# The weight rings start at the activations' offset within 512 bytes: 288 unused bytes ahead of them

## What is computed

```python
for l in range(DEPTH):                        # DEPTH = 2
    h = rms_norm(x, norm_mix[l])
    proj = h @ w_in[l]                        # 1024 x 5120
    ...
    x = x + mixed @ w_out[l]
    h = rms_norm(x, norm_ffn[l])
    x = x + conv_ffn(h, w_up[l], conv_w[l], conv_b[l], w_down[l])
x = rms_norm(x, norm_final)
proj = rmsnorm(x, norm_mix_w_2) @ w_in_2
...
x = x + mix @ w_out_2
u = relu(rmsnorm(x, norm_mlp_w_2) @ w_ff1_2)
x = x + (u * u) @ w_ff2_2
return rmsnorm(x, final_norm_w_2)
```

## The kernel before

| buffer | line | starts at | modulo 512 |
|---|---|---|---|
| xt, xg_hi, xg_lo, hid_both | 407 to 410 | 16512, 24704, 32896, 41088 | 128 |
| consts | 411 | 65664 | 128 |
| cs | 415 | 87264 | 224 |
| scratch | 419 | 92000 | 352 |
| raw, w_hi, w_lo | 420 to 422 | 151904, 176480, 201056 | 352 |

## Time and profile before

### The profile page before, as it was taken

The page is one execution under the profiler, slowest core; times in us unless marked ns, Lnnn a source line. Parts: engine busy times, 40 slices in busy tenths (PEclk is TensorE's granted clock), DMA queues, the critical chain, the costliest instruction groups (busy, mean ns, idle before and its releaser), DMA issues.

```text
span 1053.9 us, 20016 instructions
## 1 busy us (share of the span) xinstructions
PE 1039.0 (99%) x8398; PEld 984.3 (93%) x8398; DVE 720.2 (68%) x1217; ACT 572.9 (54%) x791; POOL 287.1 (27%) x179
## 2 busy tenths in 40 slices
PE   8999999999999999999999999999899999999997
PEld 7999998999999899999999989998899999899996
DVE  5762248887687775322878967877887779666663
ACT  6454466655355645445665635566548865343443
POOL 0376665100000137666640000013300035101120
PEclk9999999999999999999999999999999999999999
DMA  9644445565654764444456576446432157664841
GB/s 310 200 161 150 160 162 160 160 219 162 223 197 126 223 212 160 137 148 153 158 166 208 160 233 201 143 139 220 121 117 86 61 181 229 190 210 129 260 162 40
DMA packets 169705, 180.11 MB, mean 171 GB/s; under 512 B 4240, under 2 KB 166416, under 8 KB 169488
## 3 DMA queue, kind: packets, MB, share of 16 engines
q1 hardware_dynamic: 169616, 178.84, 53.0%
HBM read 177.78 MB, written 1.05 MB: 170 GB/s over the span
## 4 chain that ended last, share of the span: by engine, by line
PE 84%; DVE 7%; ACT 4%; POOL 2%; issue 2%; DMA 1%; SPq 0%; POOLq 0%; ACTq 0%; DVEq 0%
PE psum L679 83%; DVE sb_w_lo L1861 2%; POOL sb_w_lo L2614 1%; ACT sb_scratch L1329 1%; ACT sb_w_hi L1329 1%; DVE sb_xg_lo L1845 1%; DVE psum L1845 1%; POOL sb_scratch L2654 1%; DMA sb_raw<-in_w_ff 1%; DMA sb_raw<-in_w_in 1%; PE psum L906 1%; DVE sb_hid_both L1936 0%; DVE sb_xt L1879 0%; DVE sb_scratch L1845 0%; DVE sb_xt L1877 0%
## 5 line engine op out<-in xcount | busy, mean ns | idle before, releaser
L1329 ACT ACTIVATE sb_w_hi<-sb_raw 128x2048 fp32r<-128x2048 f32 (+3 forms) x185 | 318.4, 1726 | 163.5 <-PE psum L679 99.0
L679 PE MATMUL psum<-sb_xg_hi,sb_w_hi 128*128 128x256 f32 x1656 | 401.8, 283 | 0.1
L679 PE MATMUL psum<-sb_xg_lo,sb_w_hi 128*128 128x256 f32 x1656 | 396.7, 279 | 0.0
L1861 DVE TENSOR_TENSOR sb_w_lo<-sb_raw,sb_w_hi 128x2048 fp32r<-128x2048 f32 (+3 forms) x150 | 305.9, 2042 | 104.7 <-ACT sb_w_hi L1329 103.8
L679 PEld LDWEIGHTS psum<-sb_xg_hi,sb_w_hi 128*128 128x128 f32 x1656 | 310.3, 187 | 3.3 <-DVE sb_xg_lo L1845 0.8
L679 PEld LDWEIGHTS psum<-sb_xg_lo,sb_w_hi 128*128 128x128 f32 x1656 | 310.7, 188 | 0.3
L679 PE MATMUL psum<-sb_xg_hi,sb_w_lo 128*128 128x256 f32 x1656 | 228.3, 280 | 0.1
L679 PE MATMUL psum<-sb_hid_both,sb_w_hi 128*128 128x512 f32 (+1 forms) x912 | 210.5, 364 | 1.3 <-DVE sb_xt L1874 0.6
L679 PEld LDWEIGHTS psum<-sb_xg_hi,sb_w_lo 128*128 128x128 f32 x1656 | 207.9, 187 | 1.0 <-DVE sb_w_lo L1861 0.3
L2614 POOL TENSOR_TENSOR sb_w_lo<-sb_raw,sb_w_hi 128x2048 fp32r<-128x2048 f32 (+1 forms) x34 | 156.0, 4595 | 107.3 <-ACT sb_w_hi L1329 97.9
L679 PEld LDWEIGHTS psum<-sb_hid_both,sb_w_hi 128*128 128x128 f32 x912 | 148.7, 188 | 23.0 <-DVE sb_hid_both L1936 1.2
(11 more groups left out here) (172 smaller groups left out, 987.3 us busy)
## 6 DMA issues: line engine op xcount, KB each, us to landing
sb_raw<-in_w_in SPq DMA_DIRECT2D x51, 1024.0 KB, 5.3
sb_raw<-in_w_up SPq DMA_DIRECT2D x44, 1024.0 KB, 5.1
sb_raw<-in_w_ff SPq DMA_DIRECT2D x21, 1024.0 KB, 5.7
sb_raw<-in_w_down SPq DMA_DIRECT2D x16, 768.0 KB, 4.8
sb_raw<-in_w_down SPq DMA_DIRECT2D x16, 640.0 KB, 4.4
sb_raw<-in_w_out SPq DMA_DIRECT2D x8, 1024.0 KB, 5.2
sb_raw<-in_w_ff SPq DMA_DIRECT2D x8, 768.0 KB, 4.5
sb_raw<-in_w_ff SPq DMA_DIRECT2D x8, 640.0 KB, 4.5
```

The source lines that it names most:

```text
L679: return nc.tensor.matmul(ps, lhsT, rhs, start=start, stop=stop, skip_group_check=True)
L1329: return nc.scalar.activation(out_, in_, func, **kw)
L1861: v.tensor_tensor(part(w_lo, s), part(raw, s), part(w_hi, s).bitcast(F32), ALU.subtract)\
```

## The change

The change declares one more buffer of 72 floats, 288 bytes, between `scratch` and `raw`. Nothing reads or writes it. The three rings behind it start 288 bytes further on, at 152192, 176768 and 201344, which is 128 modulo 512. No instruction is added, removed or moved.

```diff
@@ -417,6 +417,7 @@
         gfg2 = sb("gfg2", KD)
         small = sb("small", 144)
         scratch = sb("scratch", SCRATCH)
+        sb("before_raw", 72)
         raw = sb("raw", SLOTS * SLAB)
         w_hi = sb("w_hi", SLOTS * SLAB, F32R)
         w_lo = sb("w_lo", SLOTS * SLAB, F32R)
```

## The result

The changed kernel takes 1070.7 us in the median of four executions (1070.4 to 1071.55), the kernel before 1057.66 beside it: a ratio of 1.0124, 95% interval 1.0107 to 1.0141. It is slower by 13 us, outside the predicted range.

What follows compares the result with a forecast made beforehand. The prediction took TensorE's matmul pace, 7920 units of 116.7 ns, to bound the kernel. Four terms of 0 left the profiled execution at 1055.6 us, 1057.6 us against the median, with a range of about 1053 to 1063 us.

Steps and rivals of the forecast that it cites:

- What bounds the kernel: TensorE, busy 1039.0 of 1053.9 us; its pace of 116.7 ns over 7920 units makes 924 us, and waits are no lever.
- Term 1: TensorE reading slabs as weights, about 6640 loads, with activations moving: the new offsets cost 0.
- a stride of two elements alone: Activations as weights: the stride was said to go with 120.0 in place of 116.7 ns a unit.
- Its bounds: Range for slabs as weights: 109.3 ns as in the transposes to 120.0 ns as in vd slabs, -59 to +24 us.
- The ports: Skill rule for TensorE: independent read ports for moving operand and weights, making the weight-read term exactly 0; the trace disagreed somewhat.
- Term 2: Slabs as the moving operand, some 600 units: 0, with a gain or loss of 2 us at most.
- Terms 3 and 4: Splits on the rings and slab loads into raw, where the chain passes through them: 0 each, 0.8 us both ways.
- The 3% on each load: Slab loads: by the skill's descriptor rule each takes 3% longer, an estimated +0.2 us for each of two chain pieces.
- Rival A: Slower TensorE pace spreads: 118.3 ns on 7920 units, +13 us, 1071 us; or +24 us, 1081 us; chance 0.17.
- Rival B: TensorE's surplus pace comes from offsets and goes: 7.4 ns on 7920 units, -59 us, 999 us; chance 0.13.
- Rival C: Unused buffer is left out or rounded away, rings lie as before, time the same; counted within no change's 0.70.

Runs made afterwards that it cites:

- e1: Kernel before plus three blocks of matmuls behind TensorE's last, moving the start of weights or stream in 32-byte steps, one block with 512 columns; 1188.23 us.
- e3: Kernel before with 288 bytes added ahead of the first buffer, so activations and rings move together; 1057.63 us, ratio 1.0000.
- e2: Kernel before with a gap of 32 bytes instead of 288 ahead of the rings, which begin at 384 modulo 512; 1071.66 us, ratio 1.0127.
- e4: Kernel before with 224 bytes ahead of the first buffer and 288 ahead of the rings, activations and rings both at 352; 1071.58 us, ratio 1.0123.
- e7: Kernel before with `raw` alone moved to the activations' offset, `w_hi` and `w_lo` back at 352 modulo 512; 1057.42 us, ratio 0.9991.
- e5: Kernel before plus matmul groups at eight distances, with 64 or 32 weight columns, or 128 behind one to five tiny matmuls; 1232.64 us.
- e8: Kernel before with a gap of 352 bytes ahead of the rings, distance 64 from the activations; 1049.65 us, ratio 0.9933.
- e11: Kernel before with `w_hi` and `w_lo` begun 108 bytes later in larger buffers, distance 76 from the activations; 1043.29 us, ratio 0.9860.
- e15: Kernel before plus matmul blocks with 128 down to 8 weight columns at distances 224, 0, 76 and 204, 256 and 512 moving columns; 1197.79 us.
- e13: Kernel before with `w_hi` and `w_lo` begun 236 bytes later in larger buffers, distance 204 from the activations; 1075.19 us, ratio 1.0159.
- e9: Kernel before plus matmul groups moving the weights' start in 4-byte steps through 256, behind one or two tiny matmuls and with 512 columns; 1659.36 us.
- e14: Kernel before with `w_hi` at +27, `w_lo` at +21 and `hid_both` at +58 elements, a distance for each form; 1046.4 us, ratio 0.9901.
- e12: Kernel before with `w_hi` and `w_lo` begun 84 bytes later in larger buffers, distance 52 from the activations; 1044.07 us, ratio 0.9869.

## Why the prediction was wrong

- **What bounds the kernel:** right. TensorE's pace is nine tenths of the time, and apart from 1.6 us of half clock it alone moved; the idle time of TensorE changed by 1 us in all.
- **Term 1, the failed step.** "Equal and unequal cost the same. I take 0" was drawn from float32 transposes. They run at 109 ns at both of the relative offsets that they have (the change moves none of their buffers), while fp32r matmuls on xg went to 120.0 ns. The transposes were matmuls of another type and another stream, with 128 columns, and their indifference said nothing of fp32r. The other argument, that neither side's own offset shows in the earlier trace rows, compared two cases that differ in the stream's width as well: by e1, a wide stream at unequal offsets happens to have the unit pace of a narrow one. The same holds for "a stride of two elements alone" from the earlier trace rows: there too the width differs, and in e1 narrow matmuls at distance 32 took 118.2 ns with no stride, so at most the rest is the stride's. Absolute addresses are indeed without effect (e3: 1.0000); their difference is not, and no two rows of the trace differed in it alone. With no row for the disputed case, 0 should not have had most of the chance.
- **Its bounds.** The upper one, the 120.0 ns of the vd slabs, is exactly what came. It came in 4944 matmuls and not in 7144 loads: +16.5 us in place of +24. The down stages mix forms and stay within a microsecond in all, and the last matrix gained 0.8 us.
- **The ports.** e2 and e4 put equal offsets modulo 256 at two places and cost 1.2 to 1.3%; e3 moves both sides and costs nothing. The Trainium skill ("SBUF — State Buffer", section "Who interferes with whom") gives TensorE two independent read ports for weights and moving operand. Read as the prediction read it, that made the term 0; the measurement is 120.0 in place of 116.7 ns, and it decides. The prediction itself had doubted the rule from the earlier trace rows, but the transposes outweighed that.
- **Term 2**, slabs moving: forecast 0 within 2 us, came -0.8 us in the last matrix.
- **Terms 3 and 4**, splits and loads: forecast 0 within 0.8 us each. e7, which moves `raw` alone, has 0.9991 (0.9977 to 1.0006). The 3% on each load that the prediction mentions doesn't show either: the median landings are 5.2, 5.1 and 5.7 us after, 5.3, 5.1 and 5.7 before. Right.
- **Rival A** was the right one: the slower step became the rule on xg. Its price of 1071 us was within 1 us, with 118.3 ns on 7920 units where the truth is 120.0 on 4944; the agreement of the sum is luck. The 118.3 itself came from rows rounded to 0.01 us over twelve matmuls; unrounded they are 117.8 ns, the second pace of distance 224, and that would have priced A at +9 us. Its picture, that weight loads and stream fall into a worse step, fits e5 and e8, where a start picks the pace. The mechanism underneath isn't shown.
- **Rival B** was wrong for this change. Its idea that part of the surplus comes from offsets was right: 113.3 ns is to be had (e11), while 109.3 never was. Its 7.4 ns set one float32 transpose of 128 columns equal to a unit of 256 fp32r columns, and no run shows that these are the same work.
- **Rival C**, that the change does nothing, is out: 34.56 us in place of 33.60 for the same matmuls.

## What to carry to other kernels

Where TensorE's fp32r matmuls are the bound, read the start-to-start distance over hundreds of them, and treat the distance of weights to stream modulo 256 bytes as a parameter of the layout: here it was worth -1.4% to +1.6% with no instruction changed. Try a few distances in the whole kernel and keep the best measured one, as neither an aligned layout nor a sweep of isolated groups foretold it (204 was good in the sweep and worst in the kernel). An edit that only moves buffers is not free by default, and rows of another type are no evidence for it.

## What the runs showed of the hardware

- fp32r matmuls of 256 columns on xg, in the kernels and in the sweeps, settled at 113.3 to 123.3 ns, by the distance of weights to stream modulo 256; no group was below 113.3, with 128 weight columns or with 8 (e15).
- One distance can have two or three paces; in e8 the pace changed at an interruption and was kept after it: at 64, 113.3 and 117.8 ns in one kernel, with executions from 1046.28 to 1057.86 us; at 204, 113.3, 120.0 and 123.3 (e13). Distance 0 with 128 weight columns had 120.0 in every group of 256 columns (e1, e5, e9, e15) and every unbroken stretch on xg after the change; with 64 columns it had 113.3.
- Four bytes can change the pace (72 and 76 in e9).
- A `w_hi` ring that begins at an odd multiple of 4 bytes costs ScalarE's split nothing (1903 ns in e11, 1902 before). GpSimd's split even became faster with both rings at distance 52, and in no other kernel (4741 ns in e14, where `w_lo` alone lies there); its group by form in e12 (before: 151.3 us, 4733 ns each):

```profile
L2614 POOL TENSOR_TENSOR sb_w_lo<-sb_raw,sb_w_hi 128x2048 fp32r<-128x2048 f32 x32 | 126.3, 3948 | 93.7 <-ACT sb_w_hi L1329 84.4 <-DVE sb_small L1845 9.2
```

Open are why a distance has several paces and how a start picks one, why mixed wide and narrow matmuls react less than those on xg, and what GpSimd gained at 52. No run here settles them.
